# A recurrent stage with packed 64-row gate weights, half-height sigmoids, staging tiles and an earlier convolution

## The reference

```python
u = centred_depthwise_conv(u, conv_w, conv_b)          # 4 taps along the sequence
h_fwd = rg_lru(u, w_rg_a[0], b_rg_a[0], w_rg_i[0], b_rg_i[0], lam[0], False)
h_bwd = rg_lru(u, w_rg_a[1], b_rg_a[1], w_rg_i[1], b_rg_i[1], lam[1], True)
y_rec = ((h_fwd + h_bwd) * gelu(y_branch)) @ w_rec_o
...
def rg_lru(u, w_a, b_a, w_i, b_i, lam, reverse):
    r_gate = sigmoid(block_diag_linear(u, w_a, b_a))    # 16 blocks of 64 x 64
    i_gate = sigmoid(block_diag_linear(u, w_i, b_i))
    log_a = -8 * r_gate * softplus(-lam)
    a, mult = exp(log_a), sqrt(max(-expm1(2 * log_a), 0))
    # h[t] = a[t] * h[t-1] + mult[t] * i_gate[t] * u[t]
```

## Time and profile before

| | |
|---|---|
| time, median of 3 runs | 3272.75 us (3266.36 to 3275.71) |
| profiled execution: its time, its span | 3274.24 us, 3272.4 us |
| busy in the span | PE 3189.6 us (97%), PEld 2551.9 (78%), DVE 1368.7 (42%), POOL 1036.2 (32%), ACT 816.8 (25%) |
| mean granted TensorE clock | 0.990 |
| recurrent stage | from 1601 us to 2006 us of the span, 8 blocks |

### The profile page before, as it was taken

How to read it: one execution, slowest core, us unless ns; L and a number is a source line. 1 busy time by engine, 2 the same in 40 slices (tenths; PEclk the granted TensorE clock), 3 DMA queues, 4 the chain that set the end, 5 groups by cost and what they waited for, 6 DMA issues and landing times.

```text
span 3272.4 us, 40434 instructions
## 1 busy us (share of the span) xinstructions
PE 3189.6 (97%) x15302; PEld 2551.9 (78%) x15302; DVE 1368.7 (42%) x1547; ACT 816.8 (25%) x1147; POOL 1036.2 (32%) x945
## 2 busy tenths in 40 slices
PE   8999999999999999999899999998999999999998
PEld 6776668886888888888677777886678888888886
DVE  7988864334421212124566563115556411111124
ACT  3006762024120201012424343014552201101011
POOL 3333323220333333333233233332134333333350
PEclk9999999999999999999999999999999999999999
DMA  3110011130111111111221223313021111111111
GB/s 134 45 46 26 2 72 46 57 97 7 52 45 51 45 52 45 51 45 51 103 71 61 71 74 119 110 45 129 13 90 59 49 48 50 47 51 45 51 65 52
DMA packets 49928, 194.11 MB, mean 59 GB/s; under 512 B 5664, under 2 KB 6304, under 8 KB 48544
## 3 DMA queue, kind: packets, MB, share of 16 engines
q1 hardware_dynamic: 43776, 152.50, 14.1%
q10 hardware_dynamic: 6048, 40.14, 3.2%
HBM read 171.12 MB, written 21.50 MB: 59 GB/s over the span
## 4 chain that ended last, share of the span: by engine, by line
PE 87%; DVE 7%; ACT 2%; issue 1%; DMA 1%; POOL 0%; SPq 0%; DVEq 0%; ACTq 0%; POOLq 0%
PE psum L453 70%; PE psum L847 3%; PE psum L552 2%; DVE cacc L1312 2%; PE psum L780 2%; PE psum L606 2%; PE psum L592 2%; PE psum L621 2%; PE psum L443 1%; PE psum L534 1%; PE psum L542 1%; PE psum L731 1%; PE psum L711 1%; ACT P L947 0%; DMA raw<-weights 0%
## 5 line engine op out<-in xcount | busy, mean ns | idle before, releaser
L453 PE MATMUL psum<-A_hi,w_hi 128*128 128x512 f32 x2176 | 681.3, 394 | 18.4 <-DVE A_lo L1289 13.3
L453 PE MATMUL psum<-A_lo,w_hi 128*128 128x512 f32 x2176 | 671.8, 390 | 0.0
L453 PE MATMUL psum<-A_hi,w_lo 128*128 128x512 f32 x2176 | 671.4, 390 | 0.0
L356 POOL TENSOR_TENSOR small<-ident 128x1 f32<-128x1 f32 x250 | 61.3, 245 | 1845.5 <-PE psum L453 1794.9
L362 POOL TENSOR_TENSOR w_lo<-raw,w_hi 128x1024 fp32r<-128x1024 f32 x234 | 589.6, 2520 | 19.6
L453 PEld LDWEIGHTS psum<-A_hi,w_hi 128*128 128x128 f32 x2176 | 409.0, 189 | 113.1 <-issue 26.7
L453 PEld LDWEIGHTS psum<-A_lo,w_hi 128*128 128x128 f32 x2176 | 409.9, 188 | 85.7
L453 PEld LDWEIGHTS psum<-A_hi,w_lo 128*128 128x128 f32 x2176 | 409.3, 188 | 85.6
L453 PE MATMUL psum<-B_hi,w_hi 128*128 128x512 f32 x1472 | 454.9, 390 | 1.8 <-DVE B_lo L1630 1.0
L453 PE MATMUL psum<-B_hi,w_lo 128*128 128x512 f32 x1472 | 453.2, 389 | 0.0
L453 PE MATMUL psum<-B_lo,w_hi 128*128 128x512 f32 x1472 | 453.1, 389 | 0.0
(11 more groups left out here) (241 smaller groups left out, 3289.3 us busy)
## 6 DMA issues: line engine op xcount, KB each, us to landing
raw<-weights SPq DMA_DIRECT2D x256, 512.0 KB, 3.4
gate_spill<-RU SPq DMA_DIRECT2D x16, 512.0 KB, 3.1
H<-x ACTq DMA_DIRECT2D x2, 2048.0 KB, 8.6
x_spill<-H ACTq DMA_DIRECT2D x1, 4096.0 KB, 13.0
R<-gate_spill ACTq DMA_DIRECT2D x8, 512.0 KB, 4.5
mixed_spill<-t ACTq DMA_DIRECT2D x8, 512.0 KB, 2.9
BE<-rel_bias ACTq DMA_DIRECT2D x8, 512.0 KB, 4.4
MIX<-mixed_spill ACTq DMA_DIRECT2D x1, 4096.0 KB, 14.6
```

Of the source, the lines that this page charges most:

```text
L453: last = pe.matmul(PJ[s][:, c:c + step], w[:, s, k, :], b[:, k, c:c + step], start=(k == 0 and i == 0), stop=(k == kblocks - 1 and i == 2))
```

## The change

`WG` holds for each direction one 128x128 tile, without zeros: rows 0 to 63 belong to one 64-feature block and rows 64 to 127 to the other, and the columns of a row hold both gates of its block, 64 each. So the four matmuls of a direction read 64 rows each and make both gates: those of rows 0 to 63 go to the first half of `PX`, those of rows 64 to 127 to the second. A small matmul of 128 rows and 64 columns precedes them. In the first half of `PX` the a gate is above and the i gate below, in the second half it is the other way round, so a sigmoid covers 64 partitions and there are eight in a block; those of the i gate write to other partitions than they read. TensorE does both gates of direction 0, half of job (q+1, 0), both gates of direction 1, which wait for all sigmoids of direction 0, and the other half of the job. On DVE the gate projections go to staging tiles `GS`, which lie in block 7 of `B_hi` and `B_lo` (block 7 itself uses `RC` and `RU`), so the convolution no longer waits for a store; the take of the second projection and the next convolution come right after the scans, before the sum Z and the product with the gelu.

```diff
@@ -192,7 +192,8 @@
         R_ = [at(f"R{i}", o_h + KIB4 * (1 + i), [SEQ]) for i in range(2)]
         I_ = [at(f"I{i}", o_h + KIB4 * (3 + i), [SEQ]) for i in range(2)]
         Z_ = [at(f"Z{i}", o_h + KIB4 * (5 + i), [SEQ]) for i in range(2)]
-        WG = [at(f"WG{i}", o_h + KIB4 * 7 + 2048 * i, [4, P]) for i in range(2)]
+        WG = [at(f"WG{i}", o_h + KIB4 * 7 + 2048 * i, [2, P]) for i in range(2)]
+        GS = [at("GS0", o_b + 28672, [SEQ]), at("GS1", o_b + 61440, [SEQ])]
         MIX, GA = at("MIX", o_a, [KB, SEQ]), at("GA", o_a + 32768, [KB, SEQ])
@@ -295,7 +296,8 @@
             def spill_gate(m, s):
 
                 sp.wait_ge(free[s], 2 * m + (r0 + 2))
-                sp.dma_start(block_of(io["gate_spill"], m + KB * s), RC[:]).then_inc(S[f"g_out{s}"], 16)
+                staged = (RC, RU)[s] if isinstance(m, int) and m == KB - 1 else GS[s]
+                sp.dma_start(block_of(io["gate_spill"], m + KB * s), staged[:]).then_inc(S[f"g_out{s}"], 16)
 
             def load_gates(m, slot):
                 sp.dma_start(WG[slot][:].rearrange("p a b -> p (a b)"), io["w_gates"][m]).then_inc(S[f"wg{slot}"], 16)
@@ -317,7 +319,7 @@
             with sp.Fori(1, 4) as i:
                 for par_ in range(2):
                     m = 2 * i + par_
-                    sp.wait_ge(S["r_gates"], 4 * m - 4)
+                    sp.wait_ge(S["r_gates"], 2 * m - 2)
                     load_gates(m, par_)
                     for s in range(2):
                         load_round(2 * m + r0, s)
@@ -772,16 +774,18 @@
                 pe.wait_ge(S["r_conv"], m + 1)
                 pe.wait_ge(S[f"wg{slot}"], (m // 2 + 1) * 16 if isinstance(m, int) else wg_value)
                 for d in range(2):
-                    for g in range(2):
-                        if d or not first:
-
-                            pe.wait_ge(S["r_sig"], 4 * m + (2 * d + g - 1))
-                        for h in range(2):
-                            last = pe.matmul(PX[:, 1024 * g + HALF * h:1024 * g + HALF * h + HALF],
-                                             WG[slot][:, 2 * d + g, :], RU[:, HALF * h:HALF * h + HALF],
+                    if d or not first:
+
+                        pe.wait_ge(S["r_sig"], 4 * m + 2 * d)
+                    pe.matmul(PX[:, 0:DH], WG[slot][:, d, :], RU[:, 0:DH], start=True, stop=True)
+                    for h in range(2):
+                        for b in range(2):
+                            rows = slice(DH * b, DH * b + DH)
+                            last = pe.matmul(PX[:, 1024 * b + HALF * h:1024 * b + HALF * h + HALF],
+                                             WG[slot][rows, d, :], RU[rows, HALF * h:HALF * h + HALF],
                                              start=True, stop=True)
-                        last.then_inc(S["r_gates"], 1)
-                job(q + 1, 0, A)
+                    last.then_inc(S["r_gates"], 1)
+                    job(q + 1, 0, A, order=[[0, 1, 2, 3], [4, 5, 6, 7]][d])
                 job(q + 1, 1, A)
 
             rec_round(0, 0, first=True)
@@ -1145,10 +1149,14 @@
                 for d in range(2):
                     if not first:
                         act.wait_ge(S["r_scan"], 2 * m + (d - 1))
-                    act.wait_ge(S["r_gates"], 4 * m + (2 * d + 1))
-                    tallies["r_sig"](act.activation(R_[d][:], PX[:, 0:SEQ], ACT.Sigmoid, bias=pcol("b_rg_a", m + 8 * d)))
-                    act.wait_ge(S["r_gates"], 4 * m + (2 * d + 2))
-                    tallies["r_sig"](act.activation(I_[d][:], PX[:, 1024:2048], ACT.Sigmoid, bias=pcol("b_rg_i", m + 8 * d)))
+                    act.wait_ge(S["r_gates"], 2 * m + (d + 1))
+                    for to, name in ((R_[d], "b_rg_a"), (I_[d], "b_rg_i")):
+                        for b in range(2):
+                            rows = slice(DH * b, DH * b + DH)
+                            at_rows = rows if name == "b_rg_a" else slice(DH - DH * b, 2 * DH - DH * b)
+                            gate = act.activation(to[rows, :], PX[at_rows, 1024 * b:1024 * b + SEQ], ACT.Sigmoid,
+                                                  bias=pcol(name, m + 8 * d)[at_rows, :])
+                        tallies["r_sig"](gate)
                 if not first:
                     rec_out_hi(m - 1)
                     act.wait_ge(S["r_lo"], m)
@@ -1170,6 +1178,7 @@
             with loop(act, 1, KB, {tallies["r_y"]: 1, tallies["r_sig"]: 4, tallies["r_z"]: 4,
                                    tallies["r_root"]: 2, tallies["r_hi"]: 1, chain: 2}) as m:
                 rec_gates(m)
+            act.wait_ge(S["g_out0"], 16 * (KB - 1))
             rec_out_hi(KB - 1)
 
             act.dma_start(acc[:], io["std_spill"]).then_inc(S["std_in"], 16)
@@ -1611,8 +1620,6 @@
             def rec_conv(m):
 
                 q = 2 * m + ROUNDS["rec_in"]
-                if not (isinstance(m, int) and m == 0):
-                    dve.wait_ge(S["g_out1"], 16 * m)
                 take(q, 0, RC[:], rstd[:])
                 dve.wait_ge(free[0], q + 1)
                 chain(dve.tensor_scalar(RC[:], RC[:], pcol("b_in", m + B_U), None, ALU.add))
@@ -1642,19 +1649,23 @@
                 for d in range(2):
                     dve.wait_ge(S["r_z"], 4 * m + (2 * d + 1))
                     tl["r_sq"](dve.scalar_tensor_tensor(Z_[d][:], T[2][:], 1.0, Z_[d][:], ALU.add, ALU.mult))
-                take(2 * m + (ROUNDS["rec_in"] + 1), 0, RC[:], rstd[:])
+                def take_gate(s):
+                    if not (first or last):
+                        dve.wait_ge(S[f"g_out{s}"], 16 * m)
+                    take(2 * m + (ROUNDS["rec_in"] + 1), s, ((RC, RU) if last else GS)[s][:], rstd[:])
+
+                take_gate(0)
                 for d in range(2):
                     dve.wait_ge(S["r_root"], 2 * m + (d + 1))
                     chain(dve.tensor_tensor(I_[d][:], I_[d][:], Z_[d][:], ALU.mult))
                     way = slice(None, None, -1 if d else 1)
                     tl["r_scan"](dve.tensor_tensor_scan(Z_[d][:, way], R_[d][:, way], I_[d][:, way], 0.0, ALU.mult, ALU.add))
+                take_gate(1)
+                if not last:
+                    rec_conv(m + 1)
                 chain(dve.tensor_tensor(Z_[0][:], Z_[0][:], Z_[1][:], ALU.add))
                 dve.wait_ge(S["r_y"], m + 1)
                 tl["r_out"](dve.tensor_tensor(Z_[0][:], Z_[0][:], acc[:], ALU.mult))
-                dve.wait_ge(S["g_out0"], 16 * m + 16)
-                take(2 * m + (ROUNDS["rec_in"] + 1), 1, RC[:], rstd[:])
-                if not last:
-                    rec_conv(m + 1)
 
             rec_conv(0)
             rec_block(0, first=True)
@@ -1662,12 +1673,15 @@
             with loop(dve, 1, KB - 1, rec_per) as m:
                 rec_block(m)
             rec_block(KB - 1, last=True)
+            dve.wait_ge(S["g_out1"], 16 * (KB - 1))
             rec_out_lo(KB - 1)
 
 
             for m in range(KB):
                 s = m % 2
                 dve.wait_ge(S["g_sig"], m + 1)
+                if m == 0:
+                    dve.wait_ge(S["g_out1"], 16 * KB)
                 if m >= 2:
                     dve.wait_ge(S[f"mixed_out{s}"], 16 * (m // 2))
                 take(ROUNDS["rec_out"] + m // 2, s, T[1 + s][:], R_[s][:])
@@ lay_out
-    gates = np.zeros((KB, P, 4, P), np.float32)
+    gates = np.zeros((KB, P, 2, P), np.float32)
...
-                gates[:, DH * b:DH * b + DH, 2 * d + g, DH * b:DH * b + DH] = w[d, b::2]
+                to = DH * (b if g == 0 else 1 - b)
+                gates[:, DH * b:DH * b + DH, d, to:to + DH] = w[d, b::2]
```

More of the change, by code:

```diff
@@ L1827, in ff @@
         return np.concatenate([part for c in range(FF_CHUNKS) for part in (u[KB * c:KB * c + KB], tiles_of(d[c]))])
+    swapped = lambda c: c.reshape(-1, 2, DH)[:, ::-1, :]
     w1, w2 = tiles_of(two("w_in")), tiles_of(two("w_in_2"))
@@ L1838, in lay_out @@
             i["conv_w"], i["conv_b"], i["conv_ln_g"], i["conv_ln_b"], i["b_in_2"], i["conv_w_2"], i["conv_b_2"],
-            i["b_rg_a_2"], i["b_rg_i_2"], i["lru_lambda_2"]]
+            i["b_rg_a_2"], swapped(i["b_rg_i_2"]), i["lru_lambda_2"]]
     params = np.concatenate([c.reshape(-1, P) for c in cols]).T
-    gates = np.zeros((KB, P, 4, P), np.float32)
+    gates = np.zeros((KB, P, 2, P), np.float32)
     for g, n in enumerate(("w_rg_a_2", "w_rg_i_2")):
@@ L1854, in lay_out @@
     return {
-        "weights": weights, "params": params, "w_gates": gates.reshape(KB, P, 4 * P), "rel_bias": rel_bias,
+        "weights": weights, "params": params, "w_gates": gates.reshape(KB, P, 2 * P), "rel_bias": rel_bias,
         "x": major(i["x"][0]), "mem": major(i["mem"][0]).reshape(P, -1),
```

## The result

The changed kernel is slower: 3327.43 us (3324.56 to 3329.68, 4 runs) against 3271.2 us of the kernel before beside it; ratio 1.0166, 95% interval 1.0153 to 1.0179. The profiled execution took 3329.6 us, 55.4 more than the one before. That it would be slower was forecast, but with +21.5 us for the +56.2 that came, and 3327 lies above the range of 3264 to 3306.

A forecast was written before the change was run, and what follows sets the result against it. TensorE was taken to bound the recurrent stage, without idle time in steady blocks. Terms: -2.0 - 0.4 + 7.2 + 4.8 + 11.9 = +21.5 us on the profiled 3274.24, so 3295.7 (median 3294); range 3264 to 3306.

The forecast's parts named there:

- What bounds the stage, and the slack: Recurrent stage: TensorE bounds it, no idle time in steady blocks; slack 3.9 us for slot 0, 0.8 for slot 1.
- Gate group 2.1 us: TensorE, one direction's packed gate matmuls: 2.1 us against 3.43, bounds 1.92 and 2.5; TensorE alone would need 47.7 a block.
- Rival (d): Gate matmuls on TensorE: 64-row ones don't overlap, a group takes 3.65, adding 25 us, 3321; chance 0.10.
- Half-height sigmoids cost 1.11: ScalarE: each 64-row sigmoid takes 1.11 us like a full-height one, so 8.9 instead of 4.5 us a block.
- rival (b): ScalarE: half-height sigmoids cost 0.6, the stall shrinks to 0.8, pitch 49.0, about -7 us, 3267; chance 0.10.
- `I*RU` at 14.4: VectorE: this instruction starts 14.4 us after a block's first gate matmul instead of 8.3, making the chain 6.1 later.
- Collisions with POOL, 0.65 + 0.5: VectorE waits for POOL's `w_hi`: 0.65 us at the low part, 0.5 at the second `L1644`; bounds 0 and 1.04 each.
- The take at 29.9, a wait of 4.0, pitch +1.2: Steady blocks: slot 0 is freed at 29.9, TensorE wants it at 25.9, waits 4.0 us; pitch 51.6 against 50.4.
- The clock, 1.7 a wait: TensorE: each wait brings half clock costing 1.7 us, bounds nothing and 3.4; seven times, 11.9 us.
- Rival (a): Steady blocks: the stall is there but the clock holds, +9.6 us, 3284; chance 0.18.
- Block 0, -2.0: First block of the recurrent stage: no low part, no stall, gains 2.0 of the 2.7 us saved on gates.
- The end, +4.8 and 1.7: End of the recurrent stage: last low part done at 44.1, +4.8 us with nothing hiding it, plus 1.7 of clock loss.

The follow-up runs named there:

- e7_takes_hold: Changed kernel with both VectorE takes moved earlier and POOL's split held until the low part is done; 3265.13 us, ratio 0.9969.
- e3: Changed kernel with two 128x1024 sigmoids a direction instead of four 64x1024, computing other values, for time alone; median 3274.65 us, ratio 1.0002.
- e2_hold: Changed kernel with POOL's splits for a block held until VectorE has done the low part in the block before; 3285.02 us, ratio 1.0039.
- e6_fill: Changed kernel with 33 useless 128x512 matmuls ahead of the first job of blocks 1 to 7, filling TensorE's wait; 3322.39 us.
- e1_takes: Changed kernel with both VectorE takes earlier: slot 0's ahead of the two L1651, slot 1's ahead of the product and scans; 3282.03 us, ratio 1.0029.
- e4_gates: Kernel before with packed gate weights, TensorE's new order and half-height sigmoids alone, without staging tiles or VectorE's new order; 3333.41 us, ratio 1.0179.
- e5_dve: Kernel before with the staging tiles and VectorE's new order alone, gates and sigmoids as before; 3271.69 us, ratio 1.0002.

## Why the prediction was wrong in size

- *What bounds the stage, and the slack*: right. Slot 0, with its 3.9 us of slack, was what decided.
- *Gate group 2.1 us*: right, 2.17, and e7_takes_hold, where TensorE never waits in a steady block, takes 48.17 for the forecast 47.7. Rival (d), that the 64-row matmuls don't overlap, is out.
- *Half-height sigmoids cost 1.11*: right, 1.12 (e3 beside the changed kernel); rival (b) is out. (Its pitch of 49.0 doesn't follow from the forecast's own terms: 25.9 + 0.8 + 21.8 is 48.5.) By the Trainium skill (ScalarE: Activation LUTs, What ACT_TABLE_LOAD costs) a pair would be some 93 ns shorter; the records show no such thing, 2.24 is twice 1.12, and a single one of 128x1024 in e3 takes 1.12 too.
- *`I*RU` at 14.4*: right, 14.8.
- *Collisions with POOL, 0.65 + 0.5*: this is the step that failed, a term of the right kind that was far too small. They measure 0.88 + 1.93 + 1.82 = 4.6 us. I let each VectorE instruction wait once, for a `w_hi`. The rows fit with engines that took turns: POOL's `w_hi` came between the two `I*RU`, its `w_lo` then waited for the second one and ran ahead of the low part; later a `w_hi` was pushed back by the first L1651, and the `w_lo` behind it was there when the second one asked. The mechanism was named and the size was four times too small. e2_hold shows the size by taking the collisions away; the turns are read from starts and ends, and no run changes them alone. Two bounds of 1.04 each were also too narrow: I bounded the collision with the long `w_lo` only for the take. The take took its own 1.23, as forecast. In this block that `w_lo` had ended before it; but the take at 1841.24, 1.22 long, has a `w_lo` beside it from 1841.84 on and isn't stretched either.
- *The take at 29.9, a wait of 4.0, pitch +1.2*: carried the error on. The take ends at 33.9 instead of 29.9, TensorE waits 7.4, and the pitch is 58.0 instead of 53.3 with the clock. Of these 4.7, 4.0 are the later take (3.5 by the collisions, 0.4 by the later `I*RU`) and 0.6 the clock.
- *The clock, 1.7 a wait*: right in kind, a bit low: 2.3 by the windows, 2.0 by e6_fill. Rival (a) is out for waits of 7.4 us. For short ones it is not: the clock stayed at 1.00 after five of six waits of 2.8 us in e2_hold and four of six of 2.6 in e1_takes, and fell to 0.50 after the others and after the 2.3 of idling at 486.7. A wait's length alone doesn't tell. No wait in the steady blocks came out at the forecast 4.0; the one of 3.8 in block 0 of e4_gates was followed by 0.50.
- *Block 0, -2.0*: -0.9 was measured, and why it is less stays open. *The end, +4.8 and 1.7*: the last low part comes 47.0 after the last gates instead of 44.1 (the same collisions), and the end is 8.5 longer.
- *Staging tiles and moved convolution bring nothing*: right, e5_dve shows it, and in the changed kernel VectorE no longer waits for `gate_spill`.

Put together: 17.0 us were forecast for blocks 1 to 6 and 46.2 came. The collisions and what follows from them account for 6 x (4.0 + 0.6) = 28 of the 29 between, the later `I*RU` for 2 of these 28; the rest is the longer half clock in blocks 1 to 3. That the forecast had the right sign was no luck: the late sigmoids, the queued take and the fall of the clock are all in the traces.

## What to carry to other kernels

When a change shifts a chain of short VectorE instructions against a periodic GpSimd job, work the collisions out instruction by instruction, and let both engines wait for each other; each one cost up to 1.93 us here, most of a `w_lo`. A take that frees a PSUM slot for TensorE belongs where its data are ready, not where it stood in a chain that has become later: moving two lines gave back 45 of 56 us. And where several delays feed one wait, taking away one can be worth far more than its own length, since collisions, wait and half clock can go away together: three single edits gave back 42 to 53 of the 56 us each.

## What the runs showed of the hardware that I had not expected

An fp32 matmul group of 64 rows can stand between jobs of another format at little cost: 0.26 us for the small matmul ahead of it and 0.52 from its last start to the next job, 0.43 of which is the last pair itself. That makes 2.17 for four pairs of 0.43.

The granted clock was 0.50 after every wait of 7.4 us, which cost 2.0 to 2.3 us each in the later blocks, but after only one of the six waits of 2.8 us in e2_hold's stage and two of the six of 2.6 us in e1_takes.

A sigmoid over 64 partitions took as long as one over 128, 1.12 us for 1024 columns.
